# Moving the products of an adaLN modulation from TensorE to VectorE in a two-block transformer kernel

## The reference, cut to what matters

```
for l in range(2):                       # first block
    x = x + hybrid_layer(x, ...)         # h = rmsnorm(x); p = h @ w_in; four branches
                                         #   (MLA, short conv, spatial gate, MoBA); y @ w_out
...
mod = silu(c) @ ada_w[i] + ada_b[i]      # c: 1024, ada_w[i]: 1024 x 6144, for i = 0, 1
shift, scale, gate, shift2, scale2, gate2 = split(mod, 6)
...
h = modulate(norm(x), shift, scale)      # neighbourhood attention at i = 0, grouped attention at i = 1
x = deepnorm(x, gate * attention(h))
h = modulate(norm(x), shift2, scale2)
x = deepnorm(x, gate2 * moe(h))
```

## Time and profile before

| what | us |
|---|---|
| median of 3 runs | 1769.64 (1768.62 to 1773.75) |
| the profiled execution, its own time | 1769.17 |
| its span, from the first to the last instruction | 1767.4 |
| PE busy | 1568.4 (89%) |
| PEld busy | 941.0 (53%) |
| DVE busy | 376.5 (21%) |
| ACT busy | 215.7 (12%) |
| POOL busy | 107.3 (6%) |

### The profile page before, as it was taken

How to read it: one execution, slowest core, us unless ns; L and a number is a source line. 1 busy time by engine, 2 the same in 40 slices (tenths; PEclk the granted TensorE clock), 3 DMA queues, 4 the chain that set the end, 5 groups by cost and what they waited for, 6 DMA issues and landing times.

```text
span 1767.4 us, 28139 instructions
## 1 busy us (share of the span) xinstructions
PE 1568.4 (89%) x12784; PEld 941.0 (53%) x12784; DVE 376.5 (21%) x971; ACT 215.7 (12%) x579; POOL 107.3 (6%) x109
## 2 busy tenths in 40 slices
PE   6999999987999789998898889689899988988984
PEld 3454445454846557554564555257465646545641
DVE  1411223111013240111011101354321110111113
ACT  2221113110014211000000000124110000000000
POOL 3102010020000020000000000210200000000001
PEclk9999999988998679999998999898899989989998
DMA  9447645563458447999999999932379999999994
GB/s 350 159 143 246 237 167 190 196 233 120 143 176 319 171 166 323 382 427 426 426 425 428 427 426 410 331 143 88 143 315 380 429 426 426 425 429 426 426 419 172
DMA packets 96889, 534.38 MB, mean 302 GB/s; under 512 B 5088, under 2 KB 7296, under 8 KB 73200
## 3 DMA queue, kind: packets, MB, share of 16 engines
q1 hardware_dynamic: 92992, 519.40, 73.3%
q0 software_dynamic: 3760, 13.00, 1.9%
HBM read 531.32 MB, written 1.05 MB: 301 GB/s over the span
## 4 chain that ended last, share of the span: by engine, by line
PE 67%; DMA 20%; DVE 5%; ACT 3%; issue 2%; SPq 1%; POOL 1%; DVEq 0%; ACTq 0%; POOLq 0%
PE bk L378 30%; DMA AR<-in_moe_w_down 19%; PE bk L768 17%; PE bk L800 7%; PE bk L810 3%; ACT AR L1590 3%; PE bk L374 3%; PE bk L414 2%; DVE AR L883 2%; PE bk L432 2%; SPq L2042 1%; PE bk L591 1%; DMA ring<-in_w_in 1%; POOL st L1906 1%; DVE sm L894 1%
## 5 line engine op out<-in xcount | busy, mean ns | idle before, releaser
L378 PE MATMUL bk<-ring,AR 128*128 128x512 f32 (+2 forms) x896 | 381.7, 585 | 15.6 <-DMA ring<-in_w_in 7.9
L768 PE MATMUL bk<-ring,AR 128*32 128x128 f32 x5120 | 307.3, 409 | 0.0
L378 PEld LDWEIGHTS bk<-ring,AR 128*128 128x128 f32 x896 | 172.6, 195 | 214.1 <-issue 200.4
L768 PEld LDWEIGHTS bk<-ring,AR 128*32 128x32 f32 x5120 | 193.2, 127 | 96.9 <-DVE AR L883 4.6
L768 PE MATMUL bk<-AR 128*32 128x128 f32 x3072 | 187.0, 409 | 0.0
L1590 ACT ACTIVATE AR<-bk 128x128 f32<-128x128 f32 (+4 forms) x147 | 60.4, 426 | 996.9 <-PE bk L768 765.8
L800 PE MATMUL bk<-AR 128*32 128x512 f32 x368 | 141.3, 679 | 45.2 <-DMA AR<-in_moe_w_down 44.5
L768 PEld LDWEIGHTS bk<-AR 128*32 128x32 f32 x3072 | 125.5, 128 | 53.8 <-DVE AR L883 4.6
L800 PE MATMUL bk<-ring,AR 128*32 128x512 f32 x656 | 148.4, 693 | 5.3 <-DMA ring<-in_moe_w_down 5.2
L883 DVE TENSOR_TENSOR AR<-bk,AR 128x128 f32<-128x128 f32 (+1 forms) x72 | 24.2, 336 | 510.0 <-ACT AR L1590 466.9
L378 PE MATMUL bk<-AR,X 128*128 128x128 f32 x512 | 124.5, 412 | 0.2
(11 more groups left out here) (138 smaller groups left out, 961.0 us busy)
## 6 DMA issues: line engine op xcount, KB each, us to landing
ring<-in_moe_w_gate SPq DMA_DIRECT2D x48, 2048.0 KB, 24.1
ring<-in_moe_w_down SPq DMA_DIRECT2D x36, 2048.0 KB, 28.8
ring<-in_moe_w_up SPq DMA_DIRECT2D x32, 2048.0 KB, 20.3
AR<-in_moe_w_up SPq DMA_DIRECT2D x32, 2048.0 KB, 29.0
ring<-in_ada_w SPq DMA_DIRECT2D x24, 2048.0 KB, 10.3
AR<-in_moe_w_down SPq DMA_DIRECT2D x20, 2048.0 KB, 28.3
AR<-in_moe_w_gate SPq DMA_DIRECT2D x16, 2048.0 KB, 16.4
ring<-in_w_in SPq DMA_DIRECT2D x12, 2048.0 KB, 8.9
```

The source lines that it names most:

```text
L378: ins = eng.matmul(o, l, r, start=i == 0, stop=i == len(pairs) - 1)
L768: ins = eng.matmul(o[32 * f:32 * f + 32, 128 * m:128 * m + 128], XG[u][:, c, 32 * j:32 * j + 32], w[:, c, f::4], start=c == 0, stop=c == N ...
```

## The change

VectorE computes a piece as eight steps of 128x512: a step of the ring slot is multiplied with one column of silu(c) and added to a half of mpart (`ada(steps)`, one tensor_scalar and seven scalar_tensor_tensor). TensorE sums over the partitions with one product with ones per piece (`total()`). VectorE reads the result back (`extract()`): for a gate one row; for the others 64 partitions of the bank are multiplied with the identity and reduced, and after the second piece the bias is added. ScalarE no longer takes part, and cbc is gone. The steps are placed by hand: whole pieces where VectorE waits for products, halves in the softmax iterations. Six pieces are summed in layer 0, seven in layer 1, nine between the qkv products and two in the neighbourhood attention.

The order of the other work changes with it. The chunk "s" comes right after "v"; the spatial gate's statistics, and GpSimd's part of them, come earlier, ahead of the conv taps; the taps wait for two chunks in place of five; the silu of two gates is told separately. The loads have lists of their own (LOADS, NA_LOADS). A slot with a piece of ada_w is now freed by VectorE's eighth step. The loads of ln_g and ln_b are issued once the conv of layer 1 is done, and `norm_columns(0)` stands behind VectorE's first modulated columns, ahead of the qkv copies.

```diff
-FILL = (("qk0", "qk1", "v0", "v1", "ada", "a0", "ada", "a1", "b0", "b1", "g0", "g1", "ada", "s0", "s1", "ada",
-         "pre", "ada", "conv", "ada", "spat", "ada", "ada", "ada"),
...
+FILL = ((("qk0",), ("qk1",), ("v0",), ("v1", "tot", "ext"), ("s0",), ("s1",),
+         ("a0", "svar", "ada"), ("a1", "svn", "ada"), ("b0", "tot", "ada"), ("b1", "ext", "ada"),
+         ("g0", "tot", "ada"), ("g1", "gates", "ext", "ada"), ("conv", "tot"), ("spat",)),
...
+NA_STEPS = (1, 1, 1, 2, 2, 1)
+NA_TOTALS = (1, 1, 1, 2, 2, 2)
+NA_FILL = (("ada",), ("ada",), ("tot", "ada"), ("ext", "ada"), ("tot",), ("ext",), (), (), (), ())
...
+            def total():
+                i, j = divmod(n_tot[0], 12)
+                n_tot[0] += 1
+                o = begin(next_bank(), "adaT", i, j)
+                pe.wait_ge(sem("ones"), 1)
+                pe.wait_ge(sem("ada"), n_tot[0])
+                end(product(o[:, :], [(ones[:, :], mpart[:, 512 * (j % 2):512 * (j % 2) + 512])]), "adaT", i, j)
...
+            def ada(steps):
+                for _ in range(steps):
+                    n, c = divmod(n_ada[0], NC)
...
+                    if not c:
+                        v.wait_ge(sem("silc"), 1)
+                        v.wait_ge(*loaded("ada", i, j))
+                        if n > 1:
+                            v.wait_ge(*filled("adaT", *divmod(n - 2, 12)))
+                        v.step(ts(acc, w, ccol[:, 0:1], ALU.mult))
+                        continue
+                    v.chain()
+                    ins = stt(acc, w, ccol[:, c:c + 1], acc, ALU.mult, ALU.add)
...
+            def extract():
...
+                free(tt(own, bank("adaT", i, j)[h, :].rearrange("p (k c) -> p k c", c=8), bcast(ident[h, h], 2, 8), ALU.mult),
+                     "adaT", i, j)
+                v.chain()
+                v.step(red(dsum[h, :], own.rearrange("p k c -> p c k"), ALU.add))
...
                 free(ts(ckT, bank("ckT", l)[:, 0:256], kvg[:, l, 0:1], ALU.mult), "ckT", l)
+                ada(8)
...
                         free(tt(xx, xx, bank("out", l, j, t)[:, :], ALU.add), "out", l, j, t)
+                        if not (j and t):
+                            if j or not t:
+                                extract()
+                            if not j:
+                                ada(8)
...
-            g.wait_ge(*filled("mT", 0, 3))
+            g.wait_ge(*filled("conv", 1))
```

More of the change, by code:

```diff
@@ L1 @@
+import itertools
 from contextlib import ExitStack
@@ L271, in put @@
                 holds[s] = name
-            n_ada = 0
+            n_ada = itertools.count()
             for l in range(DEPTH):
-                put(("in", l, "cq"), RING)
-                for f in FILL[l]:
+                for f in LOADS[l]:
                     if f == "ada":
[L278 to L283, removed]
-            for i in range(DEPTH):
[L285 to L289, removed]
+                        put(("ada", *divmod(next(n_ada), 12)), RING)
+                    else:
+                        put(("out", l, f) if f in (0, 1) else ("in", l, f), RING)
+            for i in range(DEPTH):
+                for j in range(3) if i else NA_LOADS:
+                    put(("ada", *divmod(next(n_ada), 12)) if j == "ada" else ("qkv", i, j), RING)
                 for k in range(EXTRA):
@@ L981, in settle @@
                 def settle():
[L982 to L1006, removed]
@@ new lines, in gated_spatial @@
+                def gated_spatial():
+                    m = sect(SU, 256)
+                    v.wait_ge(sem("ggc"), l + 1)
+                    v.wait_ge(sem("in2"), 16 * (8 + DEPTH))
+                    v.wait_ge(*filled("spat", l))
+                    for t in range(NT):
+                        ins = tt(m[:, t, :].rearrange("p (g d) -> p g d", g=4),
+                                 bank("spat", l)[:, 256 * t:256 * t + 256].rearrange("p (g d) -> p g d", g=4),
+                                 bcast(sgb[:, l, :], 2, 64), ALU.add)
+                        if t:
+                            free(ins, "spat", l)
+                        else:
+                            v.step(ins)
+                    v.chain()
+                    v.step(tt(Y[:, :, 512:768], sect(GC, 256), m, ALU.mult))
@@ L1040, in first_layer @@
                     rope_tables()
-                    v.wait_ge(sem("silc"), 1)
-                    v.tell(eng.tensor_copy(cbc, bcast(ccol[:, :], 2, 32)), sem("cbc"), 1)
+                else:
+                    extract()
+                    ada(8)
                 v.wait_ge(*filled("in", l, "cq", 1))
@@ L1955, in first_layer @@
                 rsqrt(st2[:, 8:24], st[:, 40:56], "rs12", l + 1)
-                for seg in ("v", "a", "b", "g", "s"):
+                g.wait_ge(sem("svar"), l + 1)
+                rsqrt(st2[:, 24:26], st[:, 60:62], "srs", l + 1)
+                svv = sect(SV, 256)
+                g.wait_ge(sem("svn"), l + 1)
+                g.step(tt(svv, svv, rowb(R_LG, 256), ALU.mult))
+                g.chain()
+                g.tell(tt(svv, svv, rowb(R_LB, 256), ALU.add), sem("sgv"), l + 1)
+                for seg in ("a", "b"):
                     for t in range(NT):
```

284 lines of the change are left out of this document (125 added, 159 removed).

## The result

The changed kernel takes 1721.45 us (median of 4 runs, 1720.2 to 1724.15) against 1769.13 of the kernel before in the same session: 0.9727 of it, with a 95% interval of 0.9706 to 0.9748. That is 47.7 us less, where 60.5 had been forecast. The profiled execution's span went from 1767.4 to 1718.9 us.

The account below looks back on a forecast made before the run. TensorE bounds the kernel up to the attention, expert-weight transfers later. Layers, qkv entry, qkv products and attention give 25 + 26 + 7 - 12.5 + 15 = 60.5 us off 1769.2: 1709 us, interval 1696 to 1722, range 1686 to 1744.

Parts of the forecast that it names:

- last sign: Up to 600 us: a gain under 45 us there, or a loss after, would make the prediction wrong.
- What bounds: TensorE's time counts ahead of the neighbourhood attention; after 600 us, transfers of expert weights, where nothing should change but shift.
- The prices: Modulation: 1.12 us per sum on TensorE; on VectorE 0.69 us per step, 1.4 per extraction, 161 us in all.
- Layers: Layers 0 and 1: gains of 25 and 26 us, with 3.7 us put for waiting and slow products in layer 0.
- Edits at nothing: Copy of cbc, ScalarE's copies and the earlier spatial gate on GpSimd: no gain or cost beyond the waits already counted.
- qkv products: Nine sums, 10.1 us on TensorE, two of them waiting about 1.2 us: a loss of 12.5, between 10 and 18.
- Neighbourhood attention: Bare length 39.4 us from the grouped attention, 56 with the new work; gain of 15 between 2 and 25.
- Held steps: GpSimd's taps hold VectorE's steps in both layers, up to 20 us; with cold attention 1722 to 1742 us, chance 0.18.
- Loads held behind VectorE: Late steps delay eleven weight loads in SP's queue; TensorE waits up to 10.3 us each, 1791 at eight; chance 0.09.

Follow-up runs that it names:

- the first experiment: ScalarE takes the exponentials of a softmax group ahead of its chunk copy, against the changed kernel: 1709.55 us.
- narrow steps: Seven of the eight VectorE steps of each piece cover 64 of 512 columns, against the changed kernel: 1712.85 us.
- the third experiment: The sum ahead of the out stage's last product goes to a free bank that VectorE has long read out, against the changed kernel: 1717.22 us.
- the fourth: The two pieces in the neighbourhood attention, their sums and extractions come two iterations later, against the changed kernel: 1724.6 us.

## Why the prediction was right, and where not

*The number.* 1721.45 us lies 12.4 us above the forecast and only half a us inside its own interval of 1696 to 1722; that it is inside at all is in part luck. The layers missed by 18.6 us, and the other stages gave 6.6 back, 3.7 of them in code that did not change. The prediction's own last sign, a gain under 45 us in the stages up to 600 us, speaks against it by a hair: there the gain is 44.8 us, though 0.2 us is far less than the scatter.

*What bounds.* TensorE up to the attention, transfers behind it: right. The time fell by what TensorE lost, less its new waits, and the last stage kept its length but for 3.7 us; of those, 2.2 are the projection's products, 27.70 us after the attention where they had 29.87 before, the same instructions.

*The prices.* 21 sums cost 1.02 to 1.13 us (1.12 forecast); the other three, at the end of the qkv products and in the attention, stood behind a wait at a granted clock of 0.50 and took 2.02 to 2.04. A piece takes about 6.0 us on VectorE (5.8): its first step only 0.47, the others 0.78 apart rather than 0.73. An extraction takes 1.8 us rather than 1.4, because its reduction takes 1.07 us where the row it was priced by, with the same 512 elements, has 0.68; the new one reads across the eight groups of columns. VectorE's busy time is 542.8 us, near the 530 forecast.

*Layers.* This is the step that failed: "I keep a wait of about 3 us and a slow stretch after it, and put 3.7 us for it and for the end of Y's chain". The wait of 3.3 us at MoBA's transposes was there as before, as foreseen, and the end of Y's chain cost 2.85 us of waiting and 1.5 us of slower transposes (3.53 for 2.05), near the 3.7 of the term. What the account left out is ScalarE: under "Edits at nothing" its part was said to be worth only the waits for its copies, and the one added settle call was not followed through its stream. That call put each chunk's copy ahead of the exponentials; by the first experiment it cost 4.5 and 8.2 us. The other part is the clock: a wait of 2 to 3 us in the middle of a layer cost up to about twice its length, since the products behind it ran slower (behind the 2.9 us by 3.4 us in the changed kernel, 1.7 with narrow steps and 3.1 with the free bank), where the forecast had priced most waits at their length. With the order mended and the waits at both ends covered, layer 0 gains 32.0 us and layer 1 30.3 against the kernel before, more than the forecast's 25 and 26; the 3.3 us at MoBA's transposes, which the forecast kept, are among them.

*qkv products.* The price of the nine sums and the waits for VectorE were right in kind: 4.3 us of waits in three places against two of 1.2, and sums of 1.02 to 1.10 in place of 1.12, with one of 2.04. Narrow steps took the waits away. Waits and sums take 13.8 us from start to start; that the stage lost only 9.9 is mostly due to the qkv products themselves, which took 82.8 us where they had taken about 86, at a granted clock of 0.99 against 0.97. That was not foreseen.

*Neighbourhood attention.* 65.6 us where about 66 were forecast, but by the wrong route. The bare length was read from the grouped attention, 39.4 us, with the clock as what would lengthen it. The grouped attention has no masks for VectorE to add; here VectorE's chain sets the first 16.5 us, and narrow steps shortened the first 46 us to 39.4. With most of the steps' work gone the stage still takes 59 us, the two sums included, so the bare length is nearer to 59 than to 39. A higher clock gained nothing in the first 16.5 us and something in the last 20; between them it is not tested.

*The rivals.* Held steps: they happen. Four steps that lie beside two GpSimd operations of layer 0 took 5.11 us where four take 3.11 elsewhere. The two are not taps but the scaling of the spatial gate, which the change moved ahead of the taps; of the 16 operations that the prediction counted as taps, eight are taps. VectorE's timeline, then GpSimd's:

```profile
93.43 5.11 DVE L872 SCALAR_TENSOR_TENSOR mpart<-ring,ccol,mpart 128x512 f32<-128x512 f32 x4
```
```profile
93.47 2.94 POOL L1900 TENSOR_TENSOR AR<-AR 128x512 f32<-128x512 f32 x2 [4.25 <-DVE AR L869]
```

GpSimd's two took 2.94 us, where two of that size later in the layer take 2.50. For VectorE it is 2 us per layer, not the 20 at the end of the range, as the taps hardly met a step; and narrow steps left TensorE's waits in the middle of the layers as they were, so it did not wait for these steps. The Trainium skill, page "SBUF — State Buffer", section "Who interferes with whom", says that a VectorE instruction with two inputs in SBUF contends with a GpSimd one that reads SBUF; this pair agrees. Loads held behind VectorE did not decide anything: SP's queue waited for VectorE's steps ten times,

```profile
SPq L2040 <- DVE mpart L872: 46.1, 10, 14.8
```

46.1 us in all, but TensorE's only wait for a ring transfer ahead of the attention is the one at the start. The sum ahead of the last out product was priced as a sum alone; it had to take a bank that VectorE reads only after a whole piece, 2.2 and 1.0 us of waiting.

What stays open: why the granted clock falls in one execution and not in another at the same place (layer 0 of the third experiment, the grouped attention of the fourth). It was seen, not tested.

## What to carry to other kernels

When work moves from one engine to another, follow the order of every stream that loses a step or gains one, also of the engine that only gets less to do: here one settle call on ScalarE cost 12.7 us, as much as narrowing nearly all of VectorE's new work gave back (12.5). A hidden wait has neighbours; taking one away pays only when the next one in line is covered too, so remove them together and read each stage by itself. And price a wait on TensorE with the slower products behind it, not with its length alone.

## What was not expected of the hardware

The grouped attention, with the same instructions and none of the change in it, took 41.4 us in one profiled execution and 54.3 in another, at mean granted clocks of 0.88 and 0.63 of 2.4 GHz. That difference of 12.9 us is larger than what most of the edits were worth, so a single total could not rank them; the stages could, read together with their waits and their clock.

A scalar_tensor_tensor of 128x512 that accumulates in place takes 0.75 us at the median and up to 1.86 us beside GpSimd, and the first step of a piece, a tensor_scalar of the same size with one tile input, takes 0.47 us.
